# Seven block products in place of eight for the two up projections of a two-layer decoder step

## The reference

```python
def conv_ffn(h, w_up, conv_w, w_down, buf):
    u, new_buf = causal_dwconv(h @ w_up, buf, conv_w)
    a, g = jnp.split(u, 2, axis=-1)
    return (jax.nn.silu(a) * g) @ w_down, new_buf
```

## Time and profile before

| what | us |
|---|---|
| median of 3 runs (2890.18 to 2890.9) | 2890.28 |
| the profiled execution, own time | 2890.9 |
| its span | 2890.9 |
| TensorE busy | 2675.3 (93%) |
| VectorE busy | 1348.3 (47%) |
| ScalarE busy | 1153.7 (40%) |
| POOL busy | 468.1 (16%) |

### The profile page before, as it was taken

How to read it: one execution, slowest core, us unless ns; L and a number is a source line. 1 busy time by engine, 2 the same in 40 slices (tenths; PEclk the granted TensorE clock), 3 DMA queues, 4 the chain that set the end, 5 groups by cost and what they waited for, 6 DMA issues and landing times.

```text
span 2890.9 us, 47469 instructions
## 1 busy us (share of the span) xinstructions
PE 2675.3 (93%) x18103; PEld 1816.1 (63%) x18103; DVE 1348.3 (47%) x2199; ACT 1153.7 (40%) x1599; POOL 468.1 (16%) x626
## 2 busy tenths in 40 slices
PE   5898988898888798999999999999999999999997
PEld 3666676655565465666666665566655666666664
DVE  8254454315899736444444113522345444443123
ACT  4665655322777624444443112211124444442111
POOL 0321303313445300111111000011100111111000
PEclk9999999999999899999999999999999999999999
DMA  3222223364000211111112111111111111111111
GB/s 129 82 74 61 66 68 118 95 188 129 1 1 1 81 51 37 51 45 49 51 51 66 51 51 35 51 51 51 47 42 44 51 51 51 51 51 66 50 50 59
DMA packets 113484, 173.20 MB, mean 60 GB/s; under 512 B 16993, under 2 KB 83922, under 8 KB 112978
## 3 DMA queue, kind: packets, MB, share of 16 engines
q1 hardware_dynamic: 92610, 150.90, 16.2%
q0 software_dynamic: 3792, 12.58, 1.3%
q10 hardware_dynamic: 16960, 8.16, 1.0%
HBM read 161.47 MB, written 14.30 MB: 61 GB/s over the span
## 4 chain that ended last, share of the span: by engine, by line
PE 74%; DVE 14%; ACT 5%; SPq 3%; issue 3%; DMA 1%; POOL 0%; ACTq 0%; DVEq 0%; POOLq 0%
PE PS L1804 62%; ACT xT L855 2%; DVE R L1552 2%; SPq L554 2%; PE PS L1784 2%; DVE R L1222 2%; PE PS L1837 2%; SPq L557 2%; DVE R L1531 1%; PE PS L1905 1%; DVE hT L1227 1%; PE PS L2072 1%; DVE R L1216 1%; PE PS L2003 1%; PE PS L2134 1%
## 5 line engine op out<-in xcount | busy, mean ns | idle before, releaser
L1804 PE MATMUL PS<-hT,R 128*128 128x344 f16 x10152 | 1486.6, 309 | 5.6 <-DVE R L530 4.4
L1804 PEld LDWEIGHTS PS<-hT,R 128*128 128x128 f16 x10152 | 993.4, 98 | 496.3 <-DVE R L530 3.4
L530 DVE SCALAR_TENSOR_TENSOR R<-W,R 128x1024 f16<-128x1024 f32 (+1 forms) x186 | 248.4, 1336 | 962.1 <-ACT R L524 961.5
L524 ACT ACTIVATE R<-W 128x1024 f16<-128x1024 f32 (+1 forms) x186 | 206.5, 1110 | 922.4 <-PE PS L1804 918.2
L1804 PE MATMUL PS<-R 128*128 128x344 f16 x3276 | 478.2, 309 | 0.0
L1804 PEld LDWEIGHTS PS<-R 128*128 128x128 f16 x3276 | 320.6, 98 | 157.2
L1700 DVE SCALAR_TENSOR_TENSOR R<-R 128x1024 f32<-128x1024 f32 x96 | 123.3, 1284 | 79.5 <-ACT R L1165 78.3
L855 ACT ACTIVATE xT<-xT 64x1024 f32<-64x1024 f32 x64 | 124.7, 1949 | 55.1 <-DMA xT<-cmp_t 54.0
L755 POOL COPY R<-R 128x2 f32 x88 | 19.2, 218 | 743.9 <-ACT R L1164 743.9
L761 POOL TENSOR_TENSOR R<-R 128x1032 f32 x44 | 94.2, 2142 | 275.3 <-ACT R L1171 275.3
L1702 DVE SCALAR_TENSOR_TENSOR R<-R 128x1024 f32<-128x1024 f32 x96 | 123.4, 1285 | 13.6 <-DVE R L1701 12.3
(11 more groups left out here) (300 smaller groups left out, 2792.7 us busy)
## 6 DMA issues: line engine op xcount, KB each, us to landing
W<-wk SPq DMA_DIRECT2D x154, 512.0 KB, 3.4
W<-wdn SPq DMA_DIRECT2D x32, 704.0 KB, 4.1
xT<-cmp_t SPq DMA_DIRECT2D x256, 64.0 KB, 1.9
xT<-x SPq DMA_DIRECT2D x16, 516.0 KB, 7.4
o_y<-hT SPq DMA_DIRECT2D x6, 688.0 KB, 3.5
o_win_s<-state_win POOLq DMA_DIRECT2D x1, 4088.0 KB, 23.8
R<-s_hgrn POOLq DMA_DIRECT2D x4, 512.0 KB, 5.6
o_hgrn_s<-R ACTq DMA_DIRECT2D x4, 512.0 KB, 3.2
```

The source lines that it names most:

```text
L524: act.activation(to[:, n, 0, 0:width], W[:, n, 0:width], ACT.Copy, scale=UNIT).then_inc(wh_here, 1)
L530: dve.scalar_tensor_tensor(to[:, n, 1, 0:width], W[:, n, 0:width], UNIT, to[:, n, 0, 0:width], ALU.mult, ALU.subtract).then_inc(w_split, 1)
L1804: ins = pe.matmul(wide(u)[:, m, :], weights[half], src[:, other, m * TW:(m + 1) * TW], start=(first and half == other == 0), stop=(last an ...
```

## The change

The first pair of tiles of an up projection is made as before. The 21 others are each treated as a 2 x 2 block problem: two blocks of 128 outputs, two halves of 512 features (`K4` = 4 feature tiles), two halves of 516 columns (`HT`). Strassen's scheme in its form with shared sums needs seven block products: P1 = A11 B11, P2 = A12 B21, P6, P5, P3, P7 and P4 of sums and differences. P1, P6, P5 and P3 accumulate one after another in the same PSUM banks, and P7 and P4 in another pair; what is needed in between is copied out. A product has 4 feature tiles x 3 half products x 2 parts of 258 columns = 24 matmuls. In PSUM order the outputs are C11 = P1 + P2, C12 = P1 + P6 + P5 + P3, C22 = P1 + P6 + P5 + P7, C21 = P1 + P6 + P7 + P4.

- Token side, once per projection: VectorE makes four differences of halves (`TF`, twelve operations of 4 x 172 columns), ScalarE their high halves; of the low halves VectorE makes two and POOL two (2064 columns each).
- Weight side, for each pair: POOL makes four sums of 512 columns (`SUMS`), ScalarE the high halves of A (1024), of three sums (1536), of the fourth (512) and of A22 (512); VectorE the four low halves.
- Results, for each pair: ScalarE copies P1, U2 = P1 + P6, U4 = U2 + P5 and C12 out of PSUM; VectorE joins C11, C22 and C21 (516 columns each, one operand in PSUM).
- Taps, silu, product and the halves of `Z2` are as before, but the row scaled by the last tap is made from the SBUF row.
- All this needs room: the residual `xT` is written to HBM ahead (eight transfers of 516 KB, `x_kept_in`) and read back behind (two of them at the end of the projection, six when the last row of `Z2` is there), and its space holds sums, rows and states. The state tables FS and FW are loaded only when the residual is out. POOL gathers the output states in one go at the end.
- Semaphores of the attention stage are shared (keys and values, `bias_in` for `tri_in`), since new ones are needed.

```diff
...
+    def up_weights(name, before, norm, s, index, following):
+        v, c, n0 = PLAN[before][0] + KD - 1, STEP[name], s * WP
+        wait_emptied(sp, v - 1)
+        for k in range(KD - 1):
+            sp.dma_start(x_kept_in[:, k, :], xT[:, k, :]).then_inc(x_kept, 16)
+        sp.wait_ge(w_split, c + 1)
+        sp.dma_start(W[:, 0, 0:D], wk8[index + 2]).then_inc(raw_in[0], 16)
+        wait_emptied(sp, v)
+        sp.dma_start(x_kept_in[:, KD - 1, :], xT[:, KD - 1, :]).then_inc(x_kept, 16)
+        sp.wait_ge(w_split, c + 2)
+        sp.dma_start(W[:, 1, 0:D], wk8[index + 3]).then_inc(raw_in[1], 16)
+        sp.wait_ge(t_here, KD * TN * (norm + 1))
+        sp.wait_ge(x_kept, 16 * KD * (s + 1))
+        states(s)
+        with sp.Fori(0, WP - 1) as i:
+            sp.wait_ge(part_lo, at(i, 4, 4 * n0 + 1))
+            sp.wait_ge(sum_here, at(i, 2, 2 * n0 + 2))
+            sp.dma_start(W[:, 0, 0:D].unsqueeze(1), wk8[ds(i * 2 + (index + 4), 1)].rearrange("a p n -> p a n")
+                         ).then_inc(raw_in[0], 16)
+            sp.wait_ge(part_lo, at(i, 4, 4 * n0 + 4))
+            sp.dma_start(W[:, 1, 0:D].unsqueeze(1), wk8[ds(i * 2 + (index + 5), 1)].rearrange("a p n -> p a n")
+                         ).then_inc(raw_in[1], 16)
+        n = n0 + WP - 1
+        sp.wait_ge(part_lo, 4 * n + 1)
+        sp.wait_ge(sum_here, 2 * n + 2)
+        sp.dma_start(W[:, 0, :], following[0]).then_inc(w_in[0], 16)
+        sp.wait_ge(part_lo, 4 * n + 4)
+        sp.dma_start(W[:, 1, :], following[1]).then_inc(w_in[1], 16)
+        for k in range(2):
+            sp.dma_start(xT[:, k, :], x_kept_in[:, k, :]).then_inc(x_in[k], 16)
...
+    def up_results(s):
+        sp.wait_ge(fo_here, s + 1)
+        sp.dma_start(o_ff[s], FO).then_inc(out_st, 16)
+        sp.wait_ge(z_here, 1 + KF * (s + 1))
+        for k in range(2, KD):
+            sp.dma_start(xT[:, k, :], x_kept_in[:, k, :]).then_inc(x_in[k], 16)
...
+        def sums(q, i=None):
+            n = n0 + q
+            for half in range(2):
+                pool.wait_ge(raw_in[half], at(i, 32, 16 * (n + 1)))
+            if n:
+                pool.wait_ge(part_lo, at(i, 8, 4 * n))
+            pool.tensor_tensor(SUMS[:, 2], W[:, 1, 0:D // 2], W[:, 1, D // 2:D], ALU.add).then_inc(s1_here, 1)
+            pool.tensor_tensor(SUMS[:, 1], W[:, 0, 0:D // 2], W[:, 1, 0:D // 2], ALU.subtract)
+            pool.wait_ge(s1_here, at(i, 2, n + 1))
+            pool.tensor_tensor(SUMS[:, 0], SUMS[:, 2], W[:, 0, 0:D // 2], ALU.subtract).then_inc(sum_here, 1)
+            pool.wait_ge(sum_here, at(i, 4, 2 * n + 1))
+            pool.tensor_tensor(SUMS[:, 3], W[:, 0, D // 2:D], SUMS[:, 0], ALU.subtract).then_inc(sum_here, 1)
...
+        def low(p, i=None):
+            row = Z2[:, ds(p if i is None else i * 2 + p, 1), :, :]
+            pool.wait_ge(zhi_here, at(i, 2, pairs + p + 1))
+            pool.tensor_tensor(row[:, :, 1, :], YF[0].unsqueeze(1), row[:, :, 0, :], ALU.subtract
+                               ).then_inc(z_here, 1)
+        def body(q, i=None, first=False, last=False):
+            if not last:
+                sums(q + 1, i)
+            copies(q, 1, i)
+            low(q, i)
+            copies(q + 1, 0, i)
...
+        pool.wait_ge(x_kept, 16 * KD * (s + 1))
+        sums(0)
+        for turn, b in enumerate((0, 2)):
+            pool.wait_ge(tm_hi, 4 * s + turn + 1)
+            pool.tensor_tensor(T2P[b][:, :, 1, :], TF[b], T2P[b][:, :, 0, :], ALU.subtract).then_inc(tm_pool, 1)
+        copies(0, 0)
+        over_pairs(pool, body)
...
+                act.wait_ge(prod_full, at(i, 2 * PRODUCTS, made(name, n, last)))
+            def tap(k):
+                t = 2 * p + k if i is None else i * 4 + (2 * p + k)
+                return FW[:, ds(t, 1), 2]
+            if not last:
+                after("p2")
+                part_a(q + 1, i)
+            silu(q, i)
+            after("p6")
+            if n:
+                act.wait_ge(c21_here, at(i, 2, n))
+            act.activation(split_in_two(HELD[1]), pair_of_banks(z[q % 2]), ACT.Copy, scale=1 / UNIT
+                           ).then_inc(u2_held, 1)
+            if first:
+                token_high(3, 3)
+            after("p5")
+            act.wait_ge(c11_here, at(i, 2, n + 1))
+            act.activation(split_in_two(HELD[0]), pair_of_banks(z[q % 2]), ACT.Copy, scale=1 / UNIT
+                           ).then_inc(u4_held, 1)
+            if last:
+                split_high(act, following, width=WCH)
+            else:
+                part_sums(q + 1, i)
+            high(q, i)
+            if not last:
+                hold_first(q + 1, i)
+            after("p3")
+            act.wait_ge(st_here, at(i, 4, 2 + tiles + 2 * p - 1))
+            act.activation(split_in_two(UF[0][:, 2 + HT:2 + TT]), pair_of_banks(z[q % 2]), ACT.Copy, scale=1 / UNIT
+                           ).then_inc(c12_here, 1)
+            if not last:
+                part_last_sum(q + 1, i)
+            act.wait_ge(c12_here, at(i, 2, n + 1))
+            act.wait_ge(z_here, at(i, 2, 1 + pairs + p))
+            act.activation(YF[0], UF[0][:, 2:2 + TT], ACT.Copy, scale=tap(0)).then_inc(yi_here, 1)
+            after("p4")
+            if last:
+                split_high(act, following + 1, width=WCH)
+            else:
+                part_22(q + 1, i)
+            act.wait_ge(c21_here, at(i, 2, n + 1))
+            act.activation(YF[1], UF[1][:, 2:2 + TT], ACT.Copy, scale=tap(1)).then_inc(yi_here, 1)
+        act.wait_ge(x_kept, 16 * KD * (s + 1))
+        if s:
...
+        part_a(0)
+        token_high(0, 0)
+        act.wait_ge(up_in, 64 + 32 * s)
         act.activation(FWD, FW[:, :, 2], ACT.Copy, scale=1 / UNIT).then_inc(fwd_here, 1)
-        act.wait_ge(fwd_here, n)
+        act.wait_ge(fwd_here, s + 1)
+        first_row(0)
+        token_high(1, 2)
+        token_high(2, 1)
+        wait_full(act, u + 1)
+        part_sums(0)
+        first_row(1)
+        hold_first(0)
+        part_last_sum(0)
+        part_22(0)
+        over_pairs(act, body)
+        silu(KF - 1)
+        high(KF - 1)
     stage_squares("mix_out", 1, 0)
-    last_tap(1, 4)
-    ffn_up("up0", 0, 0)
+    ffn_up("up0", 0, 0, 0)
...
+        def body(q, i=None, first=False, last=False):
+            n, p = n0 + q, q + 1
+            t = [2 * p + k if i is None else i * 4 + (2 * p + k) for k in range(2)]
...
+            after("p2")
+            dve.wait_ge(p1_held, at(i, 2, n + 1))
+            dve.wait_ge(st_here, at(i, 4, 2 + tiles + 2 * p - 1))
+            joined(UF[0][:, 2:2 + HT], quad, HELD[0]).then_inc(c11_here, 1)
+            product(q, i)
+            if first:
+                token_low(4, 3)
+            if not last:
+                low_a(q + 1, i)
+            after("p7")
+            dve.wait_ge(u4_held, at(i, 2, n + 1))
+            dve.wait_ge(st_here, at(i, 4, 2 + tiles + 2 * p))
+            joined(UF[1][:, 2 + HT:2 + TT], 2, HELD[0]).then_inc(c22_here, 1)
+            if last:
+                split_low(dve, following, width=WCH)
+            else:
+                low_sums(q + 1, i)
+            dve.wait_ge(yi_here, at(i, 4, 2 * n + 1))
+            tap(YF[0], UF[0], old(t[0]), weight(t[0]), 1)
+            after("p4")
+            dve.wait_ge(u2_held, at(i, 2, n + 1))
+            joined(UF[1][:, 2:2 + HT], 2, HELD[1]).then_inc(c21_here, 1)
+            own.settle()
+            tap(YF[0], UF[0], old(t[0]), weight(t[0]), 0, y_here)
+            if last:
+                split_low(dve, following + 1, width=WCH)
+            else:
+                low_last(q + 1, i)
+            dve.wait_ge(yi_here, at(i, 4, 2 * n + 2))
+            taps(YF[1], UF[1], old(t[1]), weight(t[1]), tg_here)
+        dve.wait_ge(t_here, KD * TN * (norm + 1))
...
+        places = ((0, 688), (516, 344), (172, 860))
...
+        def sums(turn, b, one, minus):
+            if turn > 1:
+                dve.wait_ge(tf_here, 12 * s + (3 if turn == 2 else 9))
+            for m, (f, g) in enumerate(places):
+                at_m = slice(m * 172, (m + 1) * 172)
+                block = {"11": rows[:, 0:K4, f:f + 172], "12": rows[:, 0:K4, g:g + 172],
+                         "21": rows[:, K4:KD, f:f + 172], "22": rows[:, K4:KD, g:g + 172],
+                         "t1": TF[0][:, :, at_m], "t2": TF[1][:, :, at_m]}
+                dve.tensor_tensor(TF[b][:, :, at_m], block[one], block[minus], ALU.subtract).then_inc(tf_here, 1)
+        sums(0, 0, "12", "11")
+        sums(1, 2, "22", "12")
+        sums(2, 1, "22", "t1")
+        sums(3, 3, "t2", "21")
+        dve.wait_ge(x_kept, 16 * KD * (s + 1))
+        for n in range(2):
+            own.up(dve.memset(UF[n][:, 0:2], 0.0))
+        own.settle()
+        dve.wait_ge(u_here, s * (2 + KD) + 1)
+        wait_emptied(dve, u)
+        taps(YF[0], UF[0], old(0), weight(0), y_here)
+        low_a(0)
+        token_low(3, 1)
+        low_sums(0)
+        dve.wait_ge(u_here, s * (2 + KD) + 2)
```

(56 more changed lines are left out.)

348 lines of the change are left out of this document (233 added, 115 removed).

## The result

The changed kernel takes 2937.4 us (median of 4 executions, 2937.1 to 2941.2) where the kernel before took 2890.6 beside it: 1.0164 times as long, 95% interval 1.0150 to 1.0179. The forecast of 2973 had the sign and lay 36 us too high. Its profiled execution spans 2935.6 us, 44.7 more than the earlier trace rows.

The account below looks back on a forecast made before the run. It took TensorE to bound the old up projections and VectorE's chain with POOL's sums the new ones. 25.4 us more per projection, 51 for both, plus 2 x 16 for the clock, made 83: 2890 + 83 = 2973 us, range 2840 to 3015.

Parts of the forecast that it names:

- TensorE's part: Matmuls in the up projections: 18.48 us a pair at 110 ns each; best case 53 us less per projection.
- What the other engines must do in a pair: Loop per pair through TensorE 5.28, ScalarE 2.3 and VectorE 11.4 us: 19.0 us without disturbance.
- VectorE's chain, not TensorE, is the longer: In a pair without disturbance, the 19.0 us loop exceeds TensorE's 18.48 us by 0.5.
- T: Time of one pair in the up projections: 19.0 plus 2.4 gives 21.4 us, bounds 19.0 and 22.6.
- VectorE and POOL exclude each other: In each pair two POOL sums delay VectorE's product and low_a by 1.2 us each, 2.4 in the loop.
- rival (b): VectorE's product gets in before POOL's first sum: 20.3 us a pair, no clock fall, 2901 us; chance 0.20.
- The clock: Granted clock falls behind 4 in 10 loop gaps, 14 us per projection, plus 2 behind the head's gap.
- The head: Start of each projection's pairs: the first P1 starts at 1145.7, a TensorE stall of 17 us.
- The tail: End of each projection: 1.0 us for the hold of U4 and 1.9 waiting for C21, 2.9 together.
- The sum: Per up projection 476.9 us, 25.4 more than 451.5; both 51, and 83 with the clock.
- Covered work: Residual transfers, state tables and copies, memsets, shared semaphores: each at nothing; the down projection's third chunk has some 4 us slack.
- Rival (a): VectorE and POOL do not meet: 19.0 us a pair, 36 us less per projection, 2819 us; chance 0.20.

Follow-up runs that it names:

- e1: Changed kernel with GpSimd's four weight sums cut to 8 of 512 columns in every pair but the first, most values left out: 2837.1 us, 18.55 us a pair.
- e4: Changed kernel with the four weight sums made by VectorE right after low_a, in place of GpSimd: 2850.9 us, 18.96 us a pair.
- e2: Changed kernel with eight constant fills on GpSimd in place of the four weight sums, values left out: 2859.6 us, 19.14 us a pair.
- e9: Changed kernel with ScalarE's high half of the product moved ahead of its high halves of three sums: 2872.0 us, 19.33 us a pair.
- e8: Changed kernel with one more unread 512-column difference on GpSimd in every pair but the first: 2904.6 us, 20.27 us a pair.
- e5: Changed kernel with VectorE's work at the stage's head reordered, low_a first and the last three token differences late: 2934.7 us, 21.32 us a pair.
- e6: Changed kernel with GpSimd's small copies of the previous pair's second row ahead of its four sums: 2918.0 us, 20.58 us a pair.

## Why the prediction was right and wrong

**TensorE's part: right.** The product behind a P1 starts 2.66 us after it, and e1's turn of 18.55 is the 18.48 that was said. The 98 ns a matmul that were estimated from the Trainium skill (TensorE: Matmul & The Clock Gate, section Back-to-back issue gap), 16.5 us a pair, do not hold here: the 2.66 us are 24 matmuls, 111 ns each.

**"What the other engines must do in a pair": the wrong loop.** Two steps failed. First, the 19.0 us: e1 shows 18.3. ScalarE's part was right (2.33), VectorE's took 10.4 us and not 11.4, above all since the taps were priced at 1.55 to 1.57 each and three of the four took 1.33 to 1.34 there. So without meetings the path is shorter than TensorE's 18.48, and "VectorE's chain, not TensorE, is the longer" is wrong. Second, this path does not set T in the kernel after: with low_a's meeting it is 19.4 there, and the other 1.84 us are the wait of L1383. What was left out is that the first scaled row waits for GpSimd's lower half, which is made in the same turn from the product of the pair before, since the scaled row takes this product's place. That wait stands in the diff, in ScalarE's program (`z_here`); the prediction doesn't name it.

**"VectorE and POOL exclude each other": the mechanism right, the place half wrong.** It decides the sign, as said: e4 takes away 2.31 of the 2.79 us that T lies above TensorE's part, e2 2.13. T was 21.27 where 21.4 was forecast, but by other terms. Of two sums ahead of low_a only one did harm (low_a 2.29, the product 1.23, so the product got in first, as rival (b) had it, and T was not its 20.3). The rest is low_sums ahead of the lower half, with the 0.85 by which high comes late; e9 takes that away alone, 1.9 us. That T came out within 0.1 of the forecast is chance: 0.7 too much for the path and 1.3 for a second meeting made up for a wait of 1.84 that was not in it. That VectorE's joins do not take turns was right, but there are three in a pair, not four: in e8 one takes 0.70 us with the lower half beside it.

**The clock: the term that failed.** 14 us per projection were added for falls in the loop. They came: in each projection 6 of 20 P1s took 4.2 to 4.5 us. In the loop they cost nothing:

```profile
1328.65 4.44 PE L2585 MATMUL PS<-hT,HM 128*128 128x258 f16 x24 [2.57 <-DVE HM L1946]
...
1349.90 2.82 PE L2585 MATMUL PS<-hT,HM 128*128 128x258 f16 x24 [0.87 <-DVE HM L1946]
```

From P1 to P1 it is 21.25 us again, and the next gap is 0.87 in place of 2.57. The fall took its 1.6 us out of the 1.84 that L1383 waits otherwise; behind this P1 it waits 0.15. "It would lie on P1 and P3, inside the loop" was the step; they lay beside it, on the path that had 1.84 to spare. The other 2, for the fall behind the head's gap, were right: P1 and P2 of the first pair took 7.39 us there in place of 5.46. Without the two 14s the forecast is 2945, 8 us from the time, by the chance just named.

**The head: 14.9 us, not 17.** The twelve differences took 21.62 us in place of 9.5 (the first five, with nothing of GpSimd beside them, come 0.79 apart, as said), so the exclusion cost 12.1 where 13 was said. **The tail**: 0.69 and 3.25, 3.9 where 2.9 was said; C21 stood behind a tap. **The sum**: with the 2 for the head's fall 27.4 per projection; 20 turns of 21.27 in place of 21.4 take 2.6 off, the head 2.1, the tail gives 1.0: 23.7, where 23.5 and 23.7 were measured. The sum closes, but its T is the one that came out by chance.

**Covered work: right.** No wait of TensorE stands behind the down projection's third chunk: its first 202.6 us run in one piece. Rival (a), 19.0 without meetings, was not far from what the same kernel does with one order changed (19.33); without the sums it is 18.55 (e1). I gave it 0.20 and did not see that an order of start decides between them.

## What to carry to other kernels

When two engines take turns at a resource, write down at each meeting who starts first and whose end the loop needs; let the one that the loop needs be ready first, if by moving a small step on a third engine ahead of a long one. A stall of an engine beside the loop pays for that engine's slow clock, up to the spare time there (1.84 us here): add a clock term only after the loop is closed through that engine, by following every wait, also those that only guard a reused buffer. And a kernel that saves TensorE work is not judged until the loop beside it is below TensorE's: here it was a loss of 1.6%, and after moves of work alone a gain of 2.3%.

## What was not expected of the hardware

- More work on an engine of the loop made the kernel faster: 1.27 us of GpSimd in each of 40 pairs, 33 us less (e8).
- The granted clock fell behind some gaps of 2.4 to 2.7 us and not behind all: behind 6 of 14 in each projection of the kernel after. Behind each of these 6 the next gap was only 0.4 to 1.1 us, and no fall came behind that. The length of the gap does not decide it: in e5 the second pair's P1 took 4.3 us behind a gap of 3.71 in the first projection and 2.81 behind one of 3.56 in the second. With gaps of 1.8 to 2.0 (e6) and of 0.6 to 0.8 (e9) it stayed at 1.00 through the loop from the third pair on.
- The second tile of the first up projection, up to which the instructions are nearly the same, ended between 1122.5 and 1132.8 us in these runs. Where an edit is worth a few us, its stage's own length tells more than the span.
